# Two output products, half of each as seven block products in place of eight, with the memory's split halves kept in DRAM meanwhile

## What is computed

```python
# first block
y = (o.astype(z.dtype) * jax.nn.silu(z)) @ w_out      # (512, 2048) @ (2048, 2048)
x = x + rmsnorm(y, g_post[i])

# each layer l of the second block
mem_n = rmsnorm_2(mem, mem_norm_g[l])                 # (256, 2048)
m_out = memory_attention(q_mem, mem_n, w_mk[l], w_mv[l])
...
y = jnp.concatenate([a_out, c_out, m_out], axis=-1) * jax.nn.silu(gate)
o = y @ w_o[l]                                        # (512, 2048) @ (2048, 2048)
x = x + rmsnorm_2(o, post_norm_g[l])
```

## Time and profile before

| | us |
|---|---|
| median of 3 runs (lowest to highest) | 2207.74 (2207.11 to 2207.95) |
| span of the profiled execution | 2207.3 |
| PE busy | 2190.0 |
| DVE busy | 1375.6 |
| ACT busy | 815.8 |
| POOL busy | 111.9 |
| the 14 chunks of the output product, each of the two times | 152.32 |

### The profile page before, as it was taken

How to read it: one execution, slowest core, us unless ns; L and a number is a source line. 1 busy time by engine, 2 the same in 40 slices (tenths; PEclk the granted TensorE clock), 3 DMA queues, 4 the chain that set the end, 5 groups by cost and what they waited for, 6 DMA issues and landing times.

```text
span 2207.3 us, 27611 instructions
## 1 busy us (share of the span) xinstructions
PE 2190.0 (99%) x10348; PEld 1823.7 (83%) x10348; DVE 1375.6 (62%) x2016; ACT 815.8 (37%) x1249; POOL 111.9 (5%) x151
## 2 busy tenths in 40 slices
PE   8999999999999999999999999999999999999998
PEld 7888888888888888888888888888888888888887
DVE  6687788874248643567677732386434677677665
ACT  6433434442235421334333532345213443335221
POOL 0100001101110100000000011101000000000000
PEclk9999999999999999999999999999999999999999
DMA  7455545452247222225444432373222253435432
GB/s 280 168 157 154 163 151 159 143 186 101 97 147 268 93 96 96 76 74 158 136 140 120 167 120 95 128 272 113 98 95 74 65 158 125 144 116 159 174 118 109
DMA packets 90141, 303.05 MB, mean 137 GB/s; under 512 B 7440, under 2 KB 48656, under 8 KB 66768
## 3 DMA queue, kind: packets, MB, share of 16 engines
q1 hardware_dynamic: 83760, 270.81, 37.5%
q10 hardware_dynamic: 4896, 17.30, 2.1%
q0 software_dynamic: 1408, 13.89, 1.7%
HBM read 253.74 MB, written 48.23 MB: 137 GB/s over the span
## 4 chain that ended last, share of the span: by engine, by line
PE 95%; DVE 2%; DMA 1%; issue 1%; ACT 0%; SPq 0%; POOL 0%; DVEq 0%; POOLq 0%; ACTq 0%
PE acc L551 72%; PE sc L551 11%; PE ov L551 5%; PE ov L715 1%; PE sc L896 1%; PE sc L897 1%; PE sc L702 1%; PE sc L701 1%; DMA raw<-w_dram 1%; DMA g<-xT_dram 0%; PE acc L736 0%; PE acc L737 0%; PE acc L570 0%; PE acc L566 0%; PE acc L740 0%
## 5 line engine op out<-in xcount | busy, mean ns | idle before, releaser
L551 PE MATMUL acc<-h_hi,hi 128*128 128x512 f32 x2240 | 876.5, 391 | 8.0 <-DVE h_lo L1479 8.0
L551 PE MATMUL acc<-h_lo,hi 128*128 128x512 f32 x2240 | 873.0, 390 | 0.0
L551 PE MATMUL acc<-h_hi,lo 128*128 128x512 f32 x2240 | 872.6, 390 | 0.0
L1387 DVE TENSOR_TENSOR lo<-raw,hi 128x2048 fp32r<-128x2048 f32 (+3 forms) x178 | 390.6, 2194 | 353.1 <-ACT hi L1006 351.3
L551 PEld LDWEIGHTS acc<-h_hi,hi 128*128 128x128 f32 x2240 | 421.1, 188 | 97.7 <-issue 11.4
L551 PEld LDWEIGHTS acc<-h_hi,lo 128*128 128x128 f32 x2240 | 421.1, 188 | 88.3
L551 PEld LDWEIGHTS acc<-h_lo,hi 128*128 128x128 f32 x2240 | 421.3, 188 | 84.9
L1006 ACT ACTIVATE hi<-raw 128x2048 fp32r<-128x2048 f32 (+3 forms) x178 | 327.5, 1840 | 398.6 <-PE acc L551 256.6
L1088 ACT ACTIVATE prob<-prob,st 128x256 f32<-128x256 f32 x128 | 63.6, 498 | 109.4 <-DVE st L1540 109.4
L1020 ACT ACTIVATE sq<-acc 128x512 f32<-128x512 f32 x32 | 19.2, 600 | 224.0 <-PE acc L551 217.1
L1330 ACT ACTIVATE prob<-sc,st 128x512 f32<-128x512 f32 x64 | 44.2, 690 | 43.6 <-DVE st L1959 43.6
(11 more groups left out here) (306 smaller groups left out, 2882.6 us busy)
## 6 DMA issues: line engine op xcount, KB each, us to landing
raw<-w_dram SPq DMA_DIRECT2D x170, 1024.0 KB, 4.9
turned<-pt SPq DMA_DIRECT2D x32, 512.0 KB, 3.2
pt<-turned SPq DMA_DIRECT2D x64, 256.0 KB, 4.9
turned<-pt SPq DMA_DIRECT2D x32, 448.0 KB, 3.0
pt<-turned SPq DMA_DIRECT2D x64, 224.0 KB, 4.1
xr<-residual ACTq DMA_DIRECT2D x16, 512.0 KB, 5.1
residual<-g ACTq DMA_DIRECT2D x16, 512.0 KB, 4.7
raw<-w_dram SPq DMA_DIRECT2D x8, 896.0 KB, 6.7
```

Of the source, the lines that this page charges most:

```text
L551: ins = pe.matmul(to, a, b, start=first and n == 0, stop=last and n == 2)
L1387: dve.tensor_tensor(lo[c.slot][:, 0:width], raw[c.slot][:, 0:width], hi[c.slot][:, 0:width].bitcast(F32), ALU.subtract).then_inc(lo_done, 1)
```

## The change

In both output products the tiles 2 to 15 are made in seven pairs (q = 1 to 7; tiles 2q and 2q + 1).

**Seven block products.** Over the first half of y's features (tiles 0 to 7) a pair is a product of 2 x 2 blocks (output tile 2q or 2q + 1; even or odd tile of y; first or second 256 tokens), and is made with seven block products in the Winograd form of Strassen in place of eight. A block product (`block_product`) is 4 times a matmul of the high weights by 512 columns (the high parts of 256 tokens and their low parts side by side) and one of the low weights by 256 columns (the high parts), which adds to the second half of the bank. So a pair has 28 matmuls of 512 columns and 28 of 256 where it had 48 of 512. Over the second half of y's features it has 48 as before (`half_product`).

**What is made for it.** POOL makes sums of y's blocks, once for each output product: 16 of 128 x 256 (`turned_sums`, four calls of four), and ACT and DVE split them (`t_hi`, `t_lo`: four of 128 x 1024 each). POOL makes four sums of weight blocks of 128 x 512 for each pair (`weight_sums`, `last_weight_sum`). The two halves of each bank are added by DVE (`fold`, 7 for each pair), the shared parts of the results by POOL (`early_fixes`, `late_fixes`, 5 of 128 x 256 for each pair), and the second half of the features is added on the way out of PSUM by DVE (2 of 128 x 512), where ACT had copied.

**Splits by parts.** A pair's chunks are c (slot 0: the blocks of the seven products) and d (slot 1: the second half of the features). c is split in seven pieces of 512 columns, d in two of 1024.

**Memory by way of DRAM.** The sums of y and their parts take the place of `m_hi` and `m_lo`. So the memory is loaded in eight pieces of 256 KB, and the high and low part of each are stored to DRAM (`memory_parts`). When the last block product has ended (chunk c of pair 7), four DMAs of 1 MB bring them to `m_all`. `memory_values(1)` waits for the first of these, `memory_keys(0)` for the other three.

The diff, cut to what moves work (`...` marks what is left out):

```diff
@@ SP
-                with sp.Fori(2, MEMORY // 2) as i:
-                    for p in range(2):
-                        load2(p, i, 2)
+                def store_m_piece(w):
+                    sp.wait_ge(m_done, l * ODD + (w + 1))
+                    sp.dma_start(m_parts[:, m_piece(w, 0)], m_part_hi[:, :].bitcast(F32)).then_inc(m_part_out, 16)
+                    sp.dma_start(m_parts[:, m_piece(w, 1)], m_part_lo[:, :].bitcast(F32)).then_inc(m_part_out, 16)
+                    sp.wait_ge(m_part_out, (l * ODD + (w + 1)) * 32)
...
+                for q in range(1, NP):
+                    load2(WO + 2 * q + 2)
+                    load2(WO + 2 * q + 3)
+                    store_m_piece(q)
+                    load_m_piece(q + 1)
+                load2(MEMORY, width=MW[0])
+                load2(MEMORY + 1, width=MW[1])
+                store_m_piece(NP)
+                sp.wait_ge(chunk_done, pair_of(l, NP)[0].n + 1)
+                for n, at in enumerate((1, 0, 2, 3)):
+                    to, src = (x.rearrange("p (s k n) -> p s k n", s=2, k=4)[:, :, at] for x in (m_all[:, :].bitcast(F32), m_parts))
+                    sp.dma_start(to, src).then_inc(m_rest_in if n else m_first_in, 16)
@@ POOL
+            def turned_sums(l, n):
+                m, half_ = T_ORDER[l][n], S // 2
+                b11, b12, b21, b22 = (g[:, (4 * m + x) * half_:(4 * m + x + 1) * half_] for x in range(4))
...
+                pool.tensor_tensor(t1, b12, b11, ALU.subtract).then_inc(t_sum, 1)
+                pool.tensor_tensor(t3, b22, b12, ALU.subtract).then_inc(t_sum, 1)
+                pool.wait_ge(t_sum, done + 2)
+                pool.tensor_tensor(t2, b22, t1, ALU.subtract).then_inc(t_sum, 1)
+                pool.wait_ge(t_sum, done + 3)
+                pool.tensor_tensor(t4, b21, t2, ALU.subtract).then_inc(t_sum, 1)
...
-                pool.dma_start(area[:, :], memT).then_inc(memory_in, 16)
-                add_squares(sqacc, sq_no(l, POSTN), KT)
+                for q in range(1, SP_):
+                    no = pair_of(l, q)[2]
+                    early_fixes(no)
...
+                    if q < NP:
+                        weight_sums(l, q + 1)
+                    late_fixes(no)
+                    if q < NP:
+                        last_weight_sum(l, q + 1)
@@ PE
+            def block_product(c, bank_, unit, src, first, last):
+                for m in range(4):
+                    both = src(m)
+                    w = slice(unit.start + m * P, unit.start + (m + 1) * P)
+                    pe.matmul(bank(bank_), hi[c.slot][:, w], both, start=first and m == 0, stop=False, skip_group_check=True)
+                    ins = pe.matmul(bank(bank_, TILES, TILES), lo[c.slot][:, w], both[:, 0, :], start=False, stop=last and m == 3,
+                                    skip_group_check=True)
+                return ins
...
+            def out_pair(l, q):
+                c, d, no = pair_of(l, q)
+                pe.wait_ge(unit_lo, no * 6 + 3)
...
+                block_product(c, 1, UNIT[0], y_block(0, 0), True, False).then_inc(product_done, 1)
+                pe.wait_ge(unit_lo, no * 6 + 4)
+                pe.wait_ge(t_low, l * 4 + 4)
...
+                block_product(c, 2, UNIT[1], t_block(1), True, False).then_inc(product_done, 1)
+                block_product(c, 3, UNIT[2], t_block(0), True, False).then_inc(product_done, 1)
+                pe.wait_ge(half_lo, no + 1)
+                pe.wait_ge(evacuated[c.slot], c.accs)
+                half_product(d, 0, acc[c.slot][:, :]).then_inc(half_done, 1)
+                pe.wait_ge(folded, no * 7 + 2)
+                block_product(c, 2, UNIT[3], t_block(2), False, False).then_inc(product_done, 1)
+                pe.wait_ge(unit_lo, no * 6 + 6)
+                pe.wait_ge(folded, no * 7 + 3)
+                block_product(c, 1, UNIT[2], y_block(1, 0), False, True).then_inc(product_done, 1)
+                block_product(c, 3, UNIT[0], y_block(1, 1), False, True).then_inc(product_done, 1)
+                pe.wait_ge(lo_done, c.n + 1)
+                pe.wait_ge(folded, no * 7 + 4)
+                block_product(c, 2, UNIT[1], t_block(3), False, True).then_inc(chunk_done, 1)
+                pe.wait_ge(lo_done, d.n + 1)
+                pe.wait_ge(evacuated[d.slot], d.accs)
+                half_product(d, 1, acc[d.slot][:, :]).then_inc(chunk_done, 1)
...
-                pe.wait_ge(m_done, l * ODD + ODD)
+                pe.wait_ge(m_first_in, l * 16 + 16)
                 memory_values(1)
                 sums(added, sq_no(l, PREN) + 2)
+                pe.wait_ge(m_rest_in, l * 48 + 48)
@@ DVE
+            def fold(to, b):
+                dve.tensor_reduce(to, bank(b).rearrange("p (s n) -> p n s", s=2), AX.X, ALU.add).then_inc(folded, 1)
```

373 lines of the change are left out of this document (319 added, 54 removed).

## The result

The changed kernel takes 2250.31 us (median of 4 runs, 2247.47 to 2251.45) beside 2207.76 us for the kernel before; the ratio is 1.0191, with a 95% interval of 1.0177 to 1.0206. The forecast was 2248. The sum came out, and in part that is luck, since errors of its terms offset one another: between the two profiled executions the output products cost 8.5 us less than forecast, the memory's way back 6.2 more, the entries 3.2 more and the rest 1.0 more. A lowered clock, for which there was no term, is 14 us of what was measured.

The account below looks back on a forecast made before the run. PE, busy 99% of the span, was taken as the bound: 2207.3 - 16.4 (columns) + 20 (pairs) + 10 + 7 (entries) + 6 (first pairs) + 14 (memory) = 2247.9, called 2248. Range 2240 to 2262 (0.45), wider 2214 to 2283.

Parts of the forecast that it names:

- the memory's way back: After each output product: PE waits for the four 1 MB DMAs, +7 us a layer, 14 together.
- the entries: Starts of the output products: POOL's sums and DVE's work delay PE, +10 us at the first, +7 at the second.
- PE's columns: PE in the 14 pairs: shorter matmuls bring a pair from 21.76 to 20.6 us, 16.4 us less.
- Where they don't fit: POOL and DVE exclude each other: In the pairs: DVE operations from SBUF to SBUF wait for POOL's whole instruction; a pair takes 22.3 us, not 20.6.
- the 1.7 us at the fold in 12 pairs: Seventh product of a pair waits for DVE's late fold, 1.7 us in each of 12 pairs: +20 us.
- 2 us of slack, no wait: Pair timetable without the exclusion: the next pair's splits are done at 18.6 us and needed at 20.6.
- turns one by one: Assumed order in which POOL's sums and DVE's SBUF operations alternate; at the first entry it gave 12.9 us.
- the first lands at T - 0.4, in time: First 1 MB memory DMA, issued 5.4 us before pair 7 ends (T), lands 0.4 us before T.
- A (the additions hide): Rival: POOL and DVE seldom meet, so the additions fit after all; 2192 to 2207 us, chance 0.13.
- B (the turns favour POOL): Rival: exclusion is real but turns favour POOL, whose sums are the longer chain; 2236 or 2227 us, chance 0.22.
- C (POOL starves): Rival: DVE keeps the port, POOL's sums come last, 4.2 us a pair; 2283 us, chance 0.15 with all above 2262.
- D (short matmuls wait for weights): Rival: a short matmul behind a long one waits for weights, so the 16.4 us are gone; 2265 us, chance 0.05.

Follow-up runs that it names:

- experiment 7: Kernel before, with only POOL's 16 sums of y's blocks added ahead of each output product, read by nothing: 2222.1 us, ratio 1.0071.
- experiment 5: Changed kernel, one edit each: y's second sums ahead of weight sums on POOL (second entry), 2248.2 us; y's low parts behind y's last tiles on DVE (first), 2245.0.
- experiments 3 and 6: Changed kernel with ACT's squares moved behind the weight copies, 2242.7 us; with POOL's sums replaced by fills, 2213.8, and 2200.5 with the memory direct and early too.

## Why the prediction was right, point by point

**PE's columns: mis-sized, mechanism right.** A pair without any wait takes 20.79 us, not 20.6, so 14 pairs give 13.6 us, not 16.4. A matmul of 512 columns with one of 256 behind it takes 0.353 us together, so the short one costs 0.126, 3 ns more than the row it was read from. The rule of the Trainium skill on the overlap of weight loads, page "TensorE: Matmul & The Clock Gate", stands in its section "The mechanism" and not in the one that the prediction names; the 0.126 us, which hold a load and 256 columns, disagree with it as the 0.123 did.

**"Where they don't fit: POOL and DVE exclude each other": true, and not the limit in most pairs.** The timetable asked what is late at the seventh product. In the first layer it is the fold, at the place named: 0.44 to 0.45 us in three pairs and 3.74 in pair 2, whose angles the timetable had taken as a mean over the pairs. In the second layer it is never the fold. There the ring through load, POOL's sums and ACT's squares takes 21.9 us. The step that failed is the 1.7 us at the fold in 12 pairs. Behind it stands "2 us of slack, no wait" for the timetable without the exclusion: the slack was counted at the start of the next pair, and not followed round from one load to the next. The products were forecast at +9.6 together and came to +1.1; 20 + 6 us for the waits of the pairs was 14.7 (1.1 + 13.6), of which 2.6 were clock. Of the 6 us for the first pairs 1.2 are there (21.45 and 21.34 us). Of the signs that the prediction names, the pair of 22 to 23.5 us failed: thirteen took 20.8 to 21.9, and one 27.1.

**The entries: right in sum (+17, measured +20.2), half right in cause.** At the first, y's sums by themselves cost 4.8 us (experiment 7), the low parts of the sums in DVE's queue 4.8 (experiment 5), and 2.6 of the wait's price is clock; these overlap in part, and what is left is not taken apart further. The prediction had "turns one by one" as its only mechanism. At the second, it had the sums alternating with DVE's split, and the second block product waiting for what is made of them. The wait that PE has comes from an order of queues: POOL waited for a chunk, ACT behind it for POOL, DVE for ACT, PE for DVE. But with that order changed (experiment 5) PE waits at the second block product, where the prediction had it, and the whole is shorter by less than its runs spread. So the forecast's cause was there too, hidden behind the other.

**The memory's way back: +14 forecast, +20.2 measured.** The step that failed is "the first lands at T - 0.4, in time". The four DMAs did not start at the end of chunk c's last product, 5.4 us before T, but when the stores of the last piece had landed: the last store was issued at 648.17 and took 4.42 us, so the first of the four DMAs went out at 652.6, 3.0 us before T (655.63), and the last at 654.54. So `memory_values(1)` waited 2.35 us, and the rest landed at T + 13.8, 0.8 us beyond the late end of what had been given. The clock took 4.5 us in the first layer and 2.1 in the second.

**No term for the clock.** Six stretches cost 14 us. A wait was priced at its length everywhere.

**The rivals.** A (the additions hide) was wrong for this kernel, and right about one thing: where the ring has room, DVE's waits for POOL cost nothing (experiments 3 and 6). B (the turns favour POOL) has 12 us for the pairs behind the first, nearer to the measured 13.5 than the forecast's 20, but its 13.7 for the entries and 14 for the memory are too low. C (POOL starves) shows once: POOL's sum at 1276.91 took 4.73 us, while four of DVE's operations ran from 1276.40 to 1280.50; in the pairs the two took turns. D (short matmuls wait for weights) is refuted by the 20.79.

## What to carry to other kernels

Before an operation count is turned into slack, follow the dependencies round from one load of a buffer to the next load of the same buffer: a ring that leaves the bound engine out can be longer than that engine's work, and no busy share shows it. Price a wait of PE of several microseconds as its length and a lowered clock on top (2.1 to 2.8 us behind each of the five waits of 3.7 us and more here), also where the trace of before shows neither. Where a saving of 1 us a step needs sums that all have to be made at the entry, the entry decides: here 13.6 us on PE stood against 20 us at two entries.
